# Hybrid decoder layer, one core: spilled queries and keys stored by SyncE in a layout by head, and loaded with half the DMAs

## The reference

```
h = x @ w_in + b_in
qa, ka, va, qb, kb, vb, qc, z = split(h)
oa = banded_attention(rope(qa), rope(ka), va, window, sinks)
ob = dilated_attention(rope(qb), rope(kb), vb)
mk, mv = split(mem @ w_mem)
oc = memory_attention(qc, mk, mv)
y = concat(rms(oa), rms(ob), rms(oc)) * g_branch * silu(z)
x = layer_norm(alpha * x + y @ w_out) * ln_gain + ln_bias
```

## Time and profile before

| | |
|---|---|
| time, median of 3 runs | 535.93 us (533.74 to 538.98) |
| profiled execution: its time, its span | 535.93 us, 534.0 us |
| TensorE busy | 507.4 us, 95% of the span |
| VectorE, ScalarE, GpSimd busy | 296.2, 250.2, 72.7 us |
| DMA queue of SyncE: packets, share of 16 engines | 38976, 31.9% |
| DMA queue of ACT: packets, share of 16 engines | 10720, 6.4% |

### The profile page before, as it was taken

The page is one execution under the profiler, slowest core; times in us unless marked ns, Lnnn a source line. Parts: engine busy times, 40 slices in busy tenths (PEclk is TensorE's granted clock), DMA queues, the critical chain, the costliest instruction groups (busy, mean ns, idle before and its releaser), DMA issues.

```text
span 534.0 us, 9893 instructions
## 1 busy us (share of the span) xinstructions
PE 507.4 (95%) x3560; PEld 467.5 (88%) x3560; DVE 296.2 (55%) x900; ACT 250.2 (47%) x532; POOL 72.7 (14%) x53
## 2 busy tenths in 40 slices
PE   4999999999999969999999989999999999999993
PEld 4999999999999858888888778998889989989982
DVE  4676545456566414443334577665756566565534
ACT  5622222021203035655656589574647465565530
POOL 0000000000000001011111000241414140311415
PEclk9999999999999989999999999999999999999998
DMA  8960435465622522333223476233232324131021
GB/s 289 375 189 12 158 119 157 160 203 196 212 80 97 175 94 92 97 90 101 51 86 90 127 265 220 69 94 100 91 97 88 99 58 140 53 127 41 0 80 79
DMA packets 49743, 66.14 MB, mean 124 GB/s; under 512 B 9248, under 2 KB 39328, under 8 KB 49696
## 3 DMA queue, kind: packets, MB, share of 16 engines
q1 hardware_dynamic: 38976, 53.45, 31.9%
q10 hardware_dynamic: 10720, 12.06, 6.4%
HBM read 50.28 MB, written 15.20 MB: 123 GB/s over the span
## 4 chain that ended last, share of the span: by engine, by line
PE 81%; DVE 5%; DMA 5%; SPq 3%; ACT 3%; issue 1%; POOLq 0%; POOL 0%; DVEq 0%; ACTq 0%
PE long_ps L854 15%; PE o_ps L821 11%; PE wide L686 7%; PE wide L688 7%; PE wide L687 7%; PE narrow L803 7%; PE long_ps L763 5%; PE long_ps L764 5%; PE long_ps L765 5%; PE wide L792 3%; PE wide L791 3%; DMA mem_raw<-in_mem_t 2%; DMA q_spill<-spill 2%; ACT prob L1005 2%; SPq L523 1%; PE wide L697 1%
## 5 line engine op out<-in xcount | busy, mean ns | idle before, releaser
L686 PE MATMUL wide<-x_hi,w_hi 128*128 128x256 f32 x320 | 89.8, 280 | 0.2
L687 PE MATMUL wide<-x_lo,w_hi 128*128 128x256 f32 x320 | 89.3, 279 | 0.0
L688 PE MATMUL wide<-x_hi,w_lo 128*128 128x256 f32 x320 | 89.3, 279 | 0.0
L1005 ACT ACTIVATE prob<-prob,nb 128x256 f32<-128x256 f32 (+7 forms) x96 | 52.9, 583 | 52.5 <-DVE nb L1283 32.4
L1018 ACT ACTIVATE prob_t<-narrow 128x512 f32<-128x512 f32 (+3 forms) x96 | 49.1, 529 | 39.9 <-PE narrow L803 39.5
L947 ACT ACTIVATE spill<-turn 128x512 fp32r<-128x512 f32 x21 | 13.3, 632 | 100.9 <-DVE turn L1163 58.0
L686 PEld LDWEIGHTS wide<-x_hi,w_hi 128*128 128x128 f32 x320 | 60.1, 188 | 0.5 <-issue 0.5
L688 PEld LDWEIGHTS wide<-x_hi,w_lo 128*128 128x128 f32 x320 | 60.2, 188 | 0.0
L687 PEld LDWEIGHTS wide<-x_lo,w_hi 128*128 128x128 f32 x320 | 59.8, 187 | 0.0
L803 PE MATMUL narrow<-ident,prob 128*128 128x128 f32 x328 | 50.5, 278 | 8.9 <-ACT prob L1005 8.6
L1365 POOL TENSOR_TENSOR g_lo<-g_raw,g_hi 128x1024 fp32r<-128x1024 f32 x6 | 14.3, 2390 | 279.3 <-ACT g_hi L952 279.3
(11 more groups left out here) (148 smaller groups left out, 1174.0 us busy)
## 6 DMA issues: line engine op xcount, KB each, us to landing
q_spill<-spill ACTq DMA_DIRECT2D x32, 256.0 KB, 2.6
q_pair<-q_spill SPq DMA_DIRECT2D x128, 64.0 KB, 1.9
w_raw<-in_w_qkv SPq DMA_DIRECT2D x12, 512.0 KB, 4.8
x_raw<-in_x_t SPq DMA_DIRECT2D x16, 256.0 KB, 8.0
g_raw<-in_w_gate SPq DMA_DIRECT2D x8, 512.0 KB, 3.4
q_pair<-q_spill SPq DMA_DIRECT2D x32, 128.0 KB, 2.8
q_pair<-q_spill SPq DMA_DIRECT2D x128, 32.0 KB, 1.8
wo_raw<-in_w_out SPq DMA_DIRECT2D x8, 512.0 KB, 4.1
```

Source lines behind the costliest of these rows:

```text
L686: pe.matmul(dst, w_hi[s][:, k, f], t_hi[:, k, cols], start=(k == 0), stop=False)
L687: pe.matmul(dst, w_hi[s][:, k, f], t_lo[:, k, cols], start=False, stop=False)
L688: mm = pe.matmul(dst, w_lo[s][:, k, f], t_hi[:, k, cols], start=False, stop=(k == KT - 1))
L1005: e = act.activation(prob[s][:, cols], src, ACT.Exp, bias=nb[:, r, hh:hh + 1])
```

## The change

The spill tensors get a layout by head: [head, 64 features, columns] for every kind. Stores move from ACT's list to SyncE's, where a job's store stands at that job's place in the loop, ahead of the key loads and the query loads. A q or qc job is stored with four DMAs (two halves by two blocks of 128 tokens) in place of two, a mk or kb job with two as before. Since a head's 64 features now lie together, a load needs one DMA for each of the two copies: key jobs are loaded with two DMAs in place of four, units of kind a and b with two in place of four, and c with two as before. The waits' counts follow.

```diff
         def spills(n):
             m = plan.turned.index(n)
-            return spilled[m % 2], 32 * (m // 2 + 1)
+            return spilled[m % 2], sum(16 * spill_parts(before) for before in plan.turned[m % 2:m + 1:2])
+            def store_turned(n):
+
+                c, i = jobs[n]
+                kind, m = kinds[c][0], plan.turned.index(n)
+                sp.wait_ge(turn_split, m + 1)
+                rows = HD if kind in ("mk", "qc") else HD // 2
+                for half in range(2):
+                    if rows == HD:
+                        where = slice(2 * half, 2 * half + 2), slice(0, HD)
+                    else:
+                        where = slice(0, GROUP), slice(half * rows, (half + 1) * rows)
+                    if kind in ("mk", "kb"):
+                        dst = (mk_spill if kind == "mk" else kb_spill[i])[where]
+                        sp.dma_start(dst, f32(spill[m % 2][:, half, :, :])).then_inc(spilled[m % 2], 16)
+                        continue
+                    for b in range(2):
+                        dst = q_spill[2 * i + b, kinds[c][3]][where]
+                        sp.dma_start(dst, f32(spill[m % 2][:, half, b, :])).then_inc(spilled[m % 2], 16)
...
             def load_turned_keys(n):
...
-                for half in range(2):
-                    for piece in range(2):
-                        cols = slice(piece * C, (piece + 1) * C)
-                        if kinds[c][0] == "mk":
-                            dst = k_c[piece * HD:(piece + 1) * HD, 2 * half:2 * half + 2, :]
-                            src = mk_spill[half, :, cols].rearrange("(h d) t -> d h t", d=HD)
-                        else:
-                            row = piece * HD + half * HD // 2
-                            dst = k_b[row:row + HD // 2, :, i * C:(i + 1) * C]
-                            src = kb_spill[i, half, :, cols].rearrange("(h d) t -> d h t", d=HD // 2)
-                        sp.dma_start(f32(dst), src).then_inc(turned_keys_in, 16)
+                for piece in range(2):
+                    sp.dma_start(f32(dst[piece * HD:(piece + 1) * HD]),
+                                 src[:, :, piece * C:(piece + 1) * C].rearrange("h d t -> d h t"))\
+                      .then_inc(turned_keys_in, 16)
             def load_queries(u):
...
+                for half in range(2):
+                    sp.dma_start(f32(q_pair[u % QS][half * HD:(half + 1) * HD, 0:n, :]),
+                                 q_spill[i, g, heads].rearrange("h d t -> d h t"))\
+                      .then_inc(q_in[u % QS], 16)
...
+                if n in plan.turned:
+                    store_turned(n)
                 before = n - 2
                 if before in plan.turned and kinds[jobs[before][0]][0] in ("mk", "kb"):
                     load_turned_keys(before)
...
-            def store_turned(n):
-
-                c, i = jobs[n]
-                kind, m = kinds[c][0], plan.turned.index(n)
-                act.wait_ge(turn_split, m + 1)
-                for half in range(2):
-                    if kind in ("mk", "kb"):
-                        dst = (mk_spill if kind == "mk" else kb_spill[i])[half].rearrange("r (c t) -> r c t", c=2)
-                    else:
-                        dst = q_spill[2 * i:2 * i + 2, kinds[c][3], half].rearrange("b r t -> r b t")
-                    act.dma_start(dst, f32(spill[m % 2][:, half, :, :])).then_inc(spilled[m % 2], 16)
...
-                        m = plan.turned.index(n)
-                        if m:
-                            store_turned(plan.turned[m - 1])
...
-            store_turned(plan.turned[-1])
             act.wait_ge(negated, 2)
+            act.wait_ge(turn_split, len(plan.turned))
...
-    q_spill = nc.dram_tensor("q_spill", (NB, 4, 2, P, 2 * P), F32, kind="Internal").ap()
-    kb_spill = nc.dram_tensor("kb_spill", (SEQ // C, 2, P, 2 * C), F32, kind="Internal").ap()
-    mk_spill = nc.dram_tensor("mk_spill", (2, P, 2 * MEM), F32, kind="Internal").ap()
+    q_spill = nc.dram_tensor("q_spill", (NB, 4, GROUP, HD, 2 * P), F32, kind="Internal").ap()
+    kb_spill = nc.dram_tensor("kb_spill", (SEQ // C, HB, HD, 2 * C), F32, kind="Internal").ap()
+    mk_spill = nc.dram_tensor("mk_spill", (HC, HD, 2 * MEM), F32, kind="Internal").ap()
```

More of the change, by code:

```diff
@@ L462, in layer, with spill_parts @@
         rotated = [n for n in plan.turned if kinds[jobs[n][0]][0] in ("kb", "q")]
+        def spill_parts(n):
+            return 2 if kinds[jobs[n][0]][0] in ("mk", "kb") else 4
         def spills(n):
             m = plan.turned.index(n)
-            return spilled[m % 2], 32 * (m // 2 + 1)
-        def queries(u):
-            return q_in[u % QS], sum(32 if UNITS[w][0] == "c" else 64 for w in range(u % QS, u + 1, QS))
+            return spilled[m % 2], sum(16 * spill_parts(before) for before in plan.turned[m % 2:m + 1:2])
         def query_job(u):
@@ L565, in load_queries @@
                 sp.wait_ge(*spills(query_job(u)))
[L566 to L571, removed]
-                    for half in range(2):
-                        row = twin * HD + half * HD // 2
-                        dst = q_pair[u % QS][row:row + HD // 2, 0:n, :]
-                        src = q_spill[i, g, half].rearrange("(h d) t -> d h t", d=HD // 2)[:, heads, :]
-                        sp.dma_start(f32(dst), src).then_inc(q_in[u % QS], 16)
+                for half in range(2):
+                    sp.dma_start(f32(q_pair[u % QS][half * HD:(half + 1) * HD, 0:n, :]),
+                                 q_spill[i, g, heads].rearrange("h d t -> d h t"))\
+                      .then_inc(q_in[u % QS], 16)
+            stored_turns, loaded_keys = [], []
             for n in range(n_jobs):
@@ L587, in _ @@
                     load_turned_keys(before)
-                if n >= QUERIES_AT:
+                if n >= QUERIES_AT and n - QUERIES_AT < n_jobs - QUERIES_AT:
                     load_queries(n - QUERIES_AT)
@@ L771, in score @@
                 q = q_pair[u % QS]
-                pe.wait_ge(*queries(u))
+                pe.wait_ge(q_in[u % QS], 32 * (u // QS + 1))
                 if u == 0:
                     pe.wait_ge(h_read, n_jobs)
-                    pe.wait_ge(turned_keys_in, 64 * (MEM // C + SEQ // C))
+                    pe.wait_ge(turned_keys_in, 32 * (MEM // C + SEQ // C))
                     last = plan.narrow["keys", len(plan.key_jobs) - 1]
```

5 lines of the change are left out of this document (4 added, 1 removed).

## The result

| | before | after |
|---|---|---|
| time, median of the runs made side by side | 537.31 us (533.74 to 538.98, 4 runs) | 552.62 us (550.84 to 553.05, 4 runs) |
| profiled execution: time, span | 535.93, 534.0 us | 550.91, 549.0 us |
| ratio, 95% interval | | 1.029 [1.023, 1.035] |

A forecast was written before the change was run, and what follows sets the result against it. TensorE, busy 95%, was taken as the bound, its one gap near the change ending with the last store's landing. The profiled 535.93 us + 19.5 for narrow stores - 0.5 for w_out loads gave 555 us; range 536.5 to 567.

The forecast's parts named there:

- Shape of the stores: Key and rotated-query stores, now with four outermost pieces, use four DMA engines, not sixteen; +19.0 us in all.
- Pricing four engines: Stores and other traffic on four engines from job 15 on: last store lands at 209.5, not 189.97, +19.5 us.
- the stores alone just exceed the period: A query job's store takes 6.1 us on four engines at 21.5 GB/s each, against a projection job's 5.65 us.
- My second end: Alternative price for the four-engine traffic: 23.4 GB/s per engine throughout, end at 202.9, +13 us.
- the second rival: Four engines keep up, above some 28 GB/s each; only the tail grows, +1 to +2 us, 537 us; chance 0.10.
- some 24, in one or two pieces: TensorE's gap between projections and attention grows from 4.93 to some 24 us, with the lower clock paid once.
- Mask_b behind the last store: At the projections' end, mask_b now follows job 30's store but lands before its first use: no cost.
- the first rival: Narrow stores spread over sixteen engines, last landing at 188.3, -1.7 us; 533.7 us in all; chance 0.14 (sixteen or eight).
- It fits: With wide-store timing, mask_b lands at 192.2 against a first use at 193.25, so nothing is charged.
- Stores moved: Stores issued by SyncE go out earlier; the 0.5 us buffer wait of job 30's rounding would go.
- Loads at w_out: w_out's third tile loads earlier, behind two query issues in place of four: -0.5 us, ends 0 and -0.6.

The follow-up runs named there:

- the first: Changed kernel with key and rotated-query stores made head by head, 32 rows outermost, eight DMAs per job from SyncE: 537.76 us, 0.999 of the kernel before.
- third: Kernel before with only the stores' issuer moved from ACT to SyncE; shape, layout and loads as before: 534.28 us, 0.996.
- seventh: Kernel before with wide stores issued by SyncE and the two prob tiles exchanged, so only unit 1 waits for the last store: 536.39 us, 0.998.
- The second: Kernel before with only the key and rotated-query stores made 4x32 outermost by padding rows, still issued by ACT: 595.31 us, 1.109.
- fourth: Kernel before with the rotated-query stores alone made 2x64 outermost by padding rows, issued by ACT: 638.04 us, 1.188.
- The fifth: Kernel before with narrow 4x32x512 stores for the four kb jobs only, issued by ACT: 549.19 us, 1.023.
- the sixth: Kernel before with a narrow 4x32x256 store for job 30, the last, only, issued by ACT: 542.17 us, 1.011.
- the ninth: Kernel before with wide stores from SyncE, prob tiles exchanged and mask_b issued ahead of the last store: 530.23 us, 0.984.

## Why the prediction was right, and where its terms were off

The forecast was 555.0 us (+3.6%), the result 552.6 (+2.9%), and the cause the one named: narrow stores confined to four engines, a queue that holds the roundings, and a last landing that comes late. The mechanism was right; that the sum came within 2.4 us is in part luck. It started from a profiled execution 1.4 us under the median time measured beside the changed kernel, so the loss itself was put at 19.0 us and measured as 15.3, and the terms below were off in both directions.

*Shape of the stores.* Right. 6,880 small packets were written down for four engines and counted; the share is 0.27. Two outermost pieces give 8,960, as computed, and 0.12. The Trainium skill, DMA: Bandwidth & Descriptors, section "Why a DMA increments its semaphore by 16 and not by 1", says that the number of engines is the largest up to 16 that divides the slowest dimension of both sides; both counts and both shares agree with it.

*Pricing four engines.* The term was +19.5 and measured +14.2. Mis-sized was its rate: 21.5 GB/s per engine came from a store that kept all sixteen busy, while four engines kept busy give 24.1 (131,072 bytes in 5.44 us, not 6.1). With that, "the stores alone just exceed the period" was wrong: in a quiet stretch they keep up, and the lag shrinks from 10.0 to 8.3 us. What decides is the other traffic of those engines before 160 us, which the sum did carry (11.7 us of weights, gates and key loads). But it isn't the whole account: the same bytes (2.385 MB for each engine) at 24.1 throughout are 99.0 us of work, and 100.5 + 99.0 + 0.5 = 200.0 would be +10, 4 us short of what came. One rate for all traffic was the second error, and it leans the other way: 24.1 holds where narrow stores are alone, 19.7 in 110 to 120 us, where wide loads cross them. My second end, 23.4 GB/s and +13, came nearer because the two errors nearly cancel in it. The threshold of the second rival, 28 GB/s, was the right kind of number: 24.1 lies under it, and the queue did build.

*TensorE* ran on to about 183 (181 forecast) and stood 22.6 us less a short stretch of scores and gate products; "some 24, in one or two pieces". One wait was not foreseen: unit 0's queries, 9.46 us, queued on the same engines. It lies within the wait for the last store, so it seems to have cost nothing by itself. The lower clock came twice, and not once; the first time it lies within the same wait.

*Mask_b behind the last store* cost nothing in this kernel, as forecast (DVE waited 2.60 us for a score at 207.47, for no DMA), but with less to spare: it was issued at 200.60 and took 6.3 us, not 3.8, so it landed 0.6 us ahead. For wide stores, as in the first rival, "It fits" with a landing at 192.2 was too hopeful. No run has that kernel, four wide stores and four loads. The mask took 4.3 to 4.7 us to land in the first, third and seventh experiments, and four loads 2.55 us, not 2.0, in the first. An estimate from these is 185.0 + 1.8 + 2.55 + 4.4 = 193.8, half a microsecond after its first use. With eight issues of one kind or the other ahead of the mask DVE did wait for it: until 194.25 and, in the times of the kernel before, 194.2 with eight query loads, and until 197.10 with eight stores. The rival's time of 533.7 is close to the 534.28 of the third experiment; its parts are not, since the missing wait and clock were not in it.

*Stores moved* had the right sign, and its number by luck: 188.3 was computed for a wide last store, and 188.27 measured. The third experiment's profile is 0.4 us behind that of the kernel before from its first rounding of a turned job (62.36 against 61.97). The wait of 0.5 us for the buffer did go (the rounding starts 0.1 us after its rotation, at 183.63). But the store goes out in two issues, 0.89 us, and not in the four of the sum, 1.8; and most of the gain is the shorter way of the last DMA, which the sum does not name.

*Loads at w_out*, -0.5 us: not there. ACT's first rounding of w_out is at 304.05 in the kernel before and 319.00 in the changed one, 14.95 later, and the others up to 15.0. Two loads are now issued ahead in place of four, but the transfer behind them takes 4.94 us and not 4.45, so the wait ends as it did. That is one transfer in each of two profiles; why it was longer was not tried.

*My expectations of the runs* missed six times in eleven. The second and fourth experiments came out slower by 28 and 8 us than the upper ends I gave: the fixed part between two serial stores was too small. The fifth missed the crossing of key and weight loads, the sixth put the tail of one narrow store at 3.5 us at most where it is 4.8, the seventh did not see mask_b as the next late transfer, and the ninth gained more than I gave it.

## What to carry to other kernels

Before a store or load is split or reshaped, read its outermost count on both sides: a count of 2 or 4 was here the number of engines that carried it, and 32 or more used all sixteen (no run shows a count between). Bytes per engine over the time of one job then tell whether a queue builds. The page shows it afterwards without any timeline: small packets fall to the outermost count k per DMA, and the share stays at k/16 while an engine waits. Before a late transfer is taken off the path, look for the one queued behind it: here most of the gain only came once mask_b had been moved ahead of the store (0.998 without, 0.984 with).

## What the runs showed of the hardware that was not expected

- The rate of one engine changes little when others stand idle: 24.1 GB/s with four kept busy, 22 with two that carry one store at a time, 21.5 with all sixteen, all in 1 KB pieces. The order isn't that of the counts, and why they differ was not tried.
- Issuing took longer behind a backlog. One narrow store DMA took 0.32 us at the least, 0.55 in the median and 2.75 at the most to issue from SyncE in the changed kernel; the four of job 19, at 122.50, took 8.1 us together. From ACT in the second experiment, with no other store under way, four took 2.24. What holds the issue was not tried.
- Between two serial narrow stores some 2.5 us pass beside their data, in every period of the second experiment from 160 us on (7.88 to 7.95 us, against 5.44 with a second store in the queue).
